# A dense unit of split-weight matmuls reordered: all products with the high part first, those with the low part last, with a wait of their own

## The reference

```python
def block(x, ...):
    x = x + 0.5 * rmsnorm(swiglu(rmsnorm(x, norm_g[0]), ffn1_w1, ffn1_w3, ffn1_w2), norm_g[1])
    mo, st = mixer(rmsnorm(x, norm_g[2]), w_in, ...)
    x = x + rmsnorm(mo, norm_g[3])
    x = x + 0.5 * rmsnorm(swiglu(rmsnorm(x, norm_g[4]), ffn2_w1, ffn2_w3, ffn2_w2), norm_g[5])
    return x, st

def swiglu(x, w1, w3, w2):
    return (jax.nn.silu(x @ w1) * (x @ w3)) @ w2
```

## Time and profile before

| | |
|---|---|
| median of 3 runs | 1237.59 us (1236.62 to 1241.89) |
| the profiled execution | 1238.54 us |
| its span in the profile | 1236.7 us |
| mean granted TensorE clock | 0.943 of full speed |
| PE busy | 1164.5 us (94%), 9019 matmuls |
| DVE busy | 534.4 us (43%) |
| ACT busy | 339.7 us (27%) |
| POOL busy | 128.1 us (10%) |
| transfers | 97.86 MB, mean 79 GB/s |

### The profile page before, as it was taken

How to read it: one execution, slowest core, us unless ns; L and a number is a source line. 1 busy time by engine, 2 the same in 40 slices (tenths; PEclk the granted TensorE clock), 3 DMA queues, 4 the chain that set the end, 5 groups by cost and what they waited for, 6 DMA issues and landing times.

```text
span 1236.7 us, 21696 instructions
## 1 busy us (share of the span) xinstructions
PE 1164.5 (94%) x9019; PEld 1125.6 (91%) x9019; DVE 534.4 (43%) x820; ACT 339.7 (27%) x426; POOL 128.1 (10%) x231
## 2 busy tenths in 40 slices
PE   6899999999999789999978999889999999999994
PEld 6899999999999779989965779879999999999994
DVE  5435334333334577733743233474333343333345
ACT  5322132221323343122530001243221222212231
POOL 0000709500000006001223100000000000000000
PEclk9999999999999889999986668979999999999997
DMA  5222222332222202221500002212222222322221
GB/s 211 76 93 86 85 86 85 87 94 91 70 93 69 91 35 69 86 69 52 130 28 32 21 17 94 86 33 77 95 85 85 86 85 86 90 94 87 76 76 72
DMA packets 30475, 97.86 MB, mean 79 GB/s; under 512 B 5848, under 2 KB 6104, under 8 KB 30296
## 3 DMA queue, kind: packets, MB, share of 16 engines
q1 hardware_dynamic: 30424, 97.14, 25.0%
HBM read 92.43 MB, written 4.70 MB: 79 GB/s over the span
## 4 chain that ended last, share of the span: by engine, by line
PE 88%; DVE 7%; ACT 2%; DMA 2%; issue 1%; DVEq 0%; SPq 0%; ACTq 0%
PE ps L1471 77%; PE ps L1561 2%; PE ps L1759 1%; DVE y L852 1%; DVE x L856 1%; DMA raw<-wout 1%; PE ps L1766 1%; PE ps L1713 1%; PE ps L1540 1%; DVE xl L805 1%; DVE wl L688 1%; PE ps L1752 1%; ACT wh L402 1%; PE ps L1739 0%; DMA raw<-w 0%
## 5 line engine op out<-in xcount | busy, mean ns | idle before, releaser
L1471 PE MATMUL ps<-xh,wh 128*128 128x272 f32 x1936 | 411.8, 295 | 31.7 <-DVE xl L805 24.5
L688 DVE TENSOR_TENSOR wl<-raw,wh 128x1024 fp32r<-128x1024 f32 (+1 forms) x169 | 205.5, 1216 | 515.3 <-ACT wh L402 514.6
L1471 PE MATMUL ps<-xl,wh 128*128 128x272 f32 x1936 | 406.6, 292 | 0.0
L1471 PE MATMUL ps<-xh,wl 128*128 128x272 f32 x1936 | 404.7, 291 | 0.0
L1471 PEld LDWEIGHTS ps<-xh,wh 128*128 128x128 f32 x1936 | 309.1, 192 | 37.8 <-issue 27.6
L1471 PEld LDWEIGHTS ps<-xl,wh 128*128 128x128 f32 x1936 | 311.1, 193 | 0.0
L1471 PEld LDWEIGHTS ps<-xh,wl 128*128 128x128 f32 x1936 | 309.8, 192 | 0.0
L402 ACT CAST wh<-raw 128x1024 fp32r<-128x1024 f32 (+1 forms) x169 | 173.9, 1029 | 485.4 <-PE ps L1471 476.5
L1471 PE MATMUL ps<-hh,wh 128*128 128x272 f32 x704 | 146.3, 289 | 0.5 <-DVE hl L703 0.5
L1471 PE MATMUL ps<-hl,wh 128*128 128x272 f32 x704 | 145.3, 288 | 0.0
L1471 PE MATMUL ps<-hh,wl 128*128 128x272 f32 x704 | 145.3, 288 | 0.0
(11 more groups left out here) (359 smaller groups left out, 711.1 us busy)
## 6 DMA issues: line engine op xcount, KB each, us to landing
raw<-w SPq DMA_DIRECT2D x120, 512.0 KB, 3.5
raw<-win SPq DMA_DIRECT2D x25, 512.0 KB, 3.5
raw<-w SPq DMA_DIRECT2D x16, 384.0 KB, 3.1
raw<-wout SPq DMA_DIRECT2D x8, 512.0 KB, 3.8
x<-xT SPq DMA_DIRECT2D x4, 544.0 KB, 6.7
o_yT<-x SPq DMA_DIRECT2D x8, 272.0 KB, 2.0
cs<-cT SPq DMA_DIRECT2D x1, 2048.0 KB, 8.1
o_sC<-cs SPq DMA_DIRECT2D x4, 512.0 KB, 2.6
```

Source lines behind the costliest of these rows:

```text
L688: V.tensor_tensor(wl[par][:, 0:cols], raw[par][:, 0:cols], wh[par][:, 0:cols].bitcast(F32), ALU.subtract).then_inc(split_done, 1)
L1471: last = mm(ps[:, bank + s, 0:HALF], w[par][:, kk * P:(kk + 1) * P], a[:, kk, s * HALF:(s + 1) * HALF], start=(kk == 0 and i == 0), stop=( ...
```

## The change

Within a unit the loop over contraction tiles is cut in two. The first loop runs over all tiles with the products of wh (4 matmuls a tile), the second over all tiles with the products of wl (2 a tile). The wait for `split_done` moves from ahead of the unit to between the loops; ahead of the unit stands a wait for `hi_done`, at the value u + 1. The waits for activation tiles (`wait_k`) stay in the first loop, and `unit_used` is signalled by the last matmul as before. The number of matmuls, of weight loads and of bytes is the same; ACT, DVE and SP run the same instructions in the same order. In the changed kernel the matmul stands on L1467, and `unit` begins its waits at L1473.

```diff
@@ -1461,25 +1461,32 @@
             mm = nc.tensor.matmul
             cnt = {"norm": 0, "sq": 0, "post": 0, "bc": 0, "acc": 0}
 
-            def unit(par, bank, n, a_hi, a_lo, wait_k=None):
-
+            def products(par, bank, w, a, kk, start, stop):
+
+                for s in range(2):
+                    last = mm(ps[:, bank + s, 0:HALF], w[par][:, kk * P:(kk + 1) * P], a[:, kk, s * HALF:(s + 1) * HALF],
+                              start=start, stop=stop)
+                return last
+
+            def unit(u, par, bank, n, a_hi, a_lo, wait_k=None):
+
+                pe.wait_ge(hi_done, u + 1)
                 for kk in range(n):
                     if wait_k:
                         wait_k(kk)
-                    for i, (w, a) in enumerate(((wh, a_hi), (wh, a_lo), (wl, a_hi))):
-                        for s in range(2):
-                            last = mm(ps[:, bank + s, 0:HALF], w[par][:, kk * P:(kk + 1) * P],
-                                      a[:, kk, s * HALF:(s + 1) * HALF], start=(kk == 0 and i == 0),
-                                      stop=(kk == n - 1 and i == 2))
+                    products(par, bank, wh, a_hi, kk, kk == 0, False)
+                    products(par, bank, wh, a_lo, kk, False, False)
+                pe.wait_ge(split_done, u + 3)
+                for kk in range(n):
+                    last = products(par, bank, wl, a_hi, kk, False, kk == n - 1)
                 last.then_inc(unit_used, 1)
 
             def ffn(u0, hb, yb, e0):
                 def up(u, h, c, wait_k=None):
 
-                    pe.wait_ge(split_done, u + c + 3)
                     if c % 2 == 0:
                         pe.wait_ge(h_ready, h + c // 2 + 1)
-                    unit((u0 + c) % 2, 2 * c, KD, xh, xl, wait_k)
+                    unit(u + c, (u0 + c) % 2, 2 * c, KD, xh, xl, wait_k)
 
                 for p, n in enumerate(PARTS):
                     if p == 0:
@@ -1501,9 +1508,8 @@
                     u0 += 2 * n
                     with pe.Fori(0, KD // 2) as i:
                         for c in range(2):
-                            pe.wait_ge(split_done, u0 + 2 * i + c + 3)
                             pe.wait_ge(y_evac, yb + 2 * i + c + 1)
-                            unit((u0 + c) % 2, 2 * c, n, hh, hl,
+                            unit(u0 + 2 * i + c, (u0 + c) % 2, 2 * c, n, hh, hl,
                                  (lambda kk: pe.wait_ge(h_lo, hb + kk + 1)) if c == 0 else None)
                     u0 += KD
                     hb += n
@@ -1693,14 +1699,13 @@
                      23: [lambda: turn(2)], 24: [lambda: turn(3), turn_sample]}
             for i in range(M_END):
                 u = MIX_BASE + i
-                pe.wait_ge(split_done, u + 3)
                 if i > 2:
                     pe.wait_ge(t_evac, i - 1)
                 if i == 2:
                     input_sums(7)
-                    unit(u % 2, 4, KD, xh, xl, lambda kk: spread(16, 6, 7, 0).then_inc(bc_done, 1) if kk == 3 else None)
+                    unit(u, u % 2, 4, KD, xh, xl, lambda kk: spread(16, 6, 7, 0).then_inc(bc_done, 1) if kk == 3 else None)
                 else:
-                    unit(u % 2, 2 * (i % 2), KD, xh, xl, (lambda kk: pe.wait_ge(xl_ready, KD + kk + 1)) if i == 0 else None)
+                    unit(u, u % 2, 2 * (i % 2), KD, xh, xl, (lambda kk: pe.wait_ge(xl_ready, KD + kk + 1)) if i == 0 else None)
                 for f in after.get(i, ()):
                     f()
 
@@ -1785,11 +1790,10 @@
 
             for m in range(KD):
                 u = OUT_BASE + m
-                pe.wait_ge(split_done, u + 3)
                 if m == 0:
                     pe.wait_ge(xf_ready, KD)
                 pe.wait_ge(y_evac, 24 + m + 1)
-                unit(u % 2, 2 * (m % 2), KD, xh, xl, (lambda kk: pe.wait_ge(xl_ready, 2 * KD + kk + 1)) if m == 0 else None)
+                unit(u, u % 2, 2 * (m % 2), KD, xh, xl, (lambda kk: pe.wait_ge(xl_ready, 2 * KD + kk + 1)) if m == 0 else None)
             post_norm()
             cnt["bc"] += 1
             ffn(FFN2_BASE, FT, 32, 3 * KD)
```

## The result

| | before | changed |
|---|---|---|
| median, measured side by side | 1241.43 us (1236.62 to 1243.26, 7 runs) | 1250.14 us (1244.71 to 1255.18, 7 runs) |
| the profiled execution | 1238.54 us | 1244.71 us |
| its span | 1236.7 us | 1242.9 us |
| mean granted clock | 0.943 | 0.943 |
| ratio of the times | | 1.0079, 95% interval 1.0048 to 1.0109 |

The change makes the kernel slower, by 0.8% (0.5% to 1.1%), which is 9.8 us (6.0 to 13.5). The two agree: 7 to 10 us are lost, where the prediction had 5.4. The forecast of 1243.0 us lies 7.1 us under the measured 1250.14, but 3.8 us of that are in the kernel before, which came out at 1241.43 beside it and at 1237.59 earlier.

The account below looks back on a forecast made before the run. The prediction took PE's dense matmul stream plus its stalls to bound the kernel. Its terms, -4.4 + 7.7 + 1.7 + 0.4 = +5.4 us, on the median of 1237.59 gave 1243.0 us, range 1239 to 1251.

Parts of the forecast that it names:

- Item 1: First layer, unit 4: no more wait for wl (2.73 us) nor slow clock behind it (1.63 us); -4.4 us.
- Item 2: First units of six down projections: PE stalls for the last hl tile, low products no longer covering it; +7.7 us.
- Item 3: Start of the second layer: low products, free between late xl tiles, now cost in full behind the last; +1.7 us.
- Item 4: Start of the mixer: the same shift, mostly absorbed because the spread in unit 2 comes sooner; +0.4 us.
- Item 5: First layer's start, output projection, other units' waits and the extra register instruction: no cost, up units still 6.00 us.
- Rival A: All 169 units: the wait and register instruction amid each cost PE time, 5.1 us, giving 1248.1 us; chance 0.12.
- Rival B: Six down projections: each new stall is followed by a slow clock, 9.8 us, giving 1252.8 us; chance 0.10.
- Rival C: First layer, unit 4: something other than wl holds it, so the gain fails, giving 1247.4 us; chance 0.06.
- Rival D: Low products, 16 in a row, each save 0.011 us of wh/wl switching: 30 us, near 1213 us; chance 0.05.

Follow-up runs that it names:

- mid_wait: Kernel before with its old product order, but both waits and the added register instruction of the changed kernel in all units; 1240.25 us, ratio 1.0003 to before.
- the second comparison: The changed kernel, unedited, measured again together with other kernels against the kernel before; 1246.4 us, ratio 1.0058.
- rest_new: Kernel before, new order only in units that never waited for activations or for the low part; 1238.82 us, ratio 0.9993 to before.
- up0_new: Kernel before, new order only in the 12 looped up units of the first layer's first part; 1234.93 us, ratio 0.9956 to before.

## Why the prediction was right or wrong

**Item 1, the one wait for wl: right.** -4.4 predicted, -4.3 measured in every profile with the new order and its own wait there. Unit 4 started at 40.51 (40.59 predicted), unit 5 at 46.55 (46.6). The part that was clock (1.63) was saved as well: unit 4 takes 6.05 us, 7.64 before.

**Item 2, six down projections: right.** +7.7 predicted, +7.55 measured; the four of depth 8 lost 7.36 - 6.04 = 1.32 and 1.25 or 1.26 (1.3 predicted), the two of depth 6 1.24 each (1.25). The last tile came 4.75 us after the unit (4.77). PE's waits there were shorter than forecast (1.0 to 1.5 us, 7.1 in all, for 1.1 to 1.8 and 8 to 9), but the units lost what was said.

**Item 3, the start of the second layer: right.** +1.7 predicted, +1.4 measured; between these two profiles the value for a clock that rises when it did before (1.45) was the better one. That this came out so close is in part luck: the first unit alone takes 13.18 to 14.29 us in the old order and 15.59 to 16.30 in the new one, and the means differ by 2.1.

**Item 4, the start of the mixer: right in kind.** Unit 1 lost 1.25 us and unit 3 nearly nothing, as the step said, the spread being what counts. -0.1 and +0.8 in two profiles, +0.4 predicted, which is less than the profiles of the old order differ among themselves (48.31 to 49.57). The 0.75 us of the spread is right (unit 2 takes 9.2 to 9.3 us up to unit 3 in the old order and 8.5 in the new); the step didn't have the 1.5 us of low clock that the shorter stall also saves where the clock would have fallen.

**Item 5, "at nothing": this step failed.** The starts of the first layer and of the output projection did stay covered (their first units take the same time in both orders, within the scatter), the waits and the register instruction did cost nothing (`mid_wait`), and no unit besides those named waited for its low weights. But the step took from this that a unit in steady state still takes 48 x 0.125 us. It takes 6.027 or 6.047 us, 0.5% more or a little over. By the table that is +0.5 and +0.8 in the up units of the first layer, +0.9 in those of the second, +0.5 in the later mixer units and +0.3 in the output projection, together **+3.0 us** that the sum lacks. With it the steps make 5.4 + 3.0 = 8.4 us, between the two measurements (9.8 and 7.2). The forecast gave "within 0.5%" the highest chance because its sum lay 0.8 us under that edge; the missing 3.0 us carry it over. This is read from the profiles. The times alone would not show it: 5.4 lies inside the second comparison's 4.1 to 10.2 us and just under the first's 6.0 to 13.5, and `rest_new`, where the spacing is nearly alone, isn't slower than before. The range of 1239 to 1251 holds the measured 1250.14.

Two numbers of the prediction don't follow from its own steps. Its bounds make 3.9 to 7.9 us, so 1241.5 to 1245.5 on the median and not 1246.5. And a spacing of 115.8 ns would not make the sum 0.7 us less: with the last tile fixed at 4.77 us, item 2 has PE stand for 4.77 - 28 x 0.1158 = 1.53 us and not 1.26, four times over, and the sum comes out about 0.5 us higher.

**Rival A fell:** `mid_wait` has its mechanism alone and is at 1.0003. What it saw in down units (6.02 to 6.03) is what up units now show, for another reason, and the price was 3.0 us and not 5.1, since the down units didn't change. **Rival B fell:** the clock was 1.00 behind all six stalls, and the first down units took the same time, in all four profiles with the new order there. But the argument against it was partly luck: it leaned on a clock of 1.00 behind a stall of 1.95 us, and behind that same stall the clock fell in four of the six profiles that have it. What the runs support is that it did not fall behind stalls of 1.0 to 1.5 us. The Trainium skill, TensorE: Matmul & The Clock Gate, "A second HAM failure mode: psum-queue depth-cycling", tells of a kernel whose frequent short idle moments between groups of matmuls make the clock swing. Six in 1240 us did not do that here. **Rival C fell** (`up0_new`). **Rival D fell:** switching between wh and wl costs nothing that 16 low products in a row would save. They run at 125.0 ns in the first layer's second part, as they did one tile at a time.

**What stays open.** First, what widens the spacing. Where a unit takes 6.027 us it lies in the 32 products of wh (125.0 to 125.8 ns), not in the 16 of wl (125.0); where it takes 6.047 the 16 are slower too (126.35). No gap stands at the middle wait, and the same loop gave 6.047 us a unit in one profile and 6.027 in another. Second, the whole against its parts. The four kernels with one kind each multiply to 1.0055 x 0.9956 x 0.9997 x 0.9993 = 1.0001, about 0 ± 6 us, and the changed kernel is at 7 to 10. In the profiles the parts do add up (-4.0 + 7.6 + 2.8 + 0.4 = 6.8 from the table of the four, 7.0 and 7.9 from the two whole ones), and the times of the single kernels each lie 1 to 3 us below their parts. Scatter of the heads' stage can do that, and I take it for the cause; an effect that comes only when all parts stand together isn't ruled out.

## What to carry to other kernels

Which product goes last in a unit is a choice of which late operand it covers: putting all products of one operand last hides that operand's lateness, and takes away the cover of the others, so count for each unit what is really late there (here `wl` once, the activations at six down projections and two stage starts) and choose the order by unit. Read such a loss as matmuls left ahead of the last arrival, times the spacing from the trace; that came out within 0.1 us at each of the six down projections. And before calling the steady state free, leave room for a spacing that changes by 0.5%: here it was 3.0 us beside a predicted sum of 5.4.

## What the hardware showed that was not expected

- The order of the products changes the pace of a stream that never waits: 6.000 or 6.013 us for 48 matmuls with wh, wh, wl in turn at each tile (125.0 or 125.3 ns), 6.027 or 6.047 with all wl last (125.6 or 126.0). Not in every place: down units take 6.027 to 6.030 in either order.
- A semaphore wait that is already met, and a register instruction, amid a stream of matmuls cost nothing that a profile shows (`mid_wait`: 6.000).
- Six stalls of 1.0 to 1.5 us in dense work left the granted clock at 1.00 each time, in each of four profiles. A stall of 1.9 us at one and the same place was followed by 1.00 in two profiles and by 0.57 to 0.70 in four, and one of 2.6 us by 0.53. One profile can't say whether such a stall costs clock.
- A sparse stage with identical code takes 121.8 to 132.8 us, by the clock that it is granted (0.71 to 0.65), and that scatter is larger than the change under study.
